# A Trainium2 transformer kernel: 1/rms applied to what leaves the products, and norms in a written order

## The chip, the cores and the metric

One program on one core of a Trainium2 chip. The metric is the device time in microseconds of one execution. The runs of the kernel before have a median of 4474.64 us (4474.46 to 4476.37, three runs).

## What is computed

A residual stream of 1024 tokens by 1024 features goes through one transformer block and two further layers. The part that the change touches is the first block:

```python
def rms_norm(x, g):
    y = x * lax.rsqrt(jnp.mean(x * x, axis=-1, keepdims=True) + RMS_EPS)
    return y * g

def swiglu(x, w_gate, w_up, w_down):
    return (jax.nn.silu(x @ w_gate) * (x @ w_up)) @ w_down

f1 = swiglu(rms_norm(x, ffn1_pre_g), ffn1_w_gate, ffn1_w_up, ffn1_w_down)   # 1024 -> 2816 -> 1024
x = x + 0.5 * rms_norm(f1, ffn1_post_g)
m = token_mixer(rms_norm(x, mix_pre_g), w_in, fox_forget_b, ..., w_out)
x = x + rms_norm(m, mix_post_g)
f2 = swiglu(rms_norm(x, ffn2_pre_g), ffn2_w_gate, ffn2_w_up, ffn2_w_down)
x = x + 0.5 * rms_norm(f2, ffn2_post_g)
```

The token mixer projects the rows with `w_in` into queries, keys and values of eight heads with a forget gate and of four differential heads (two softmaxes each, the second subtracted with a factor lambda, partly rotated queries and keys), and into eight gate columns. The logarithm of the gate's sigmoid is summed up over the tokens and added to the logits of the first eight heads. The heads' outputs go through `w_out`. Behind the block come an even layer (a gated linear recurrence and a state space scan) and an odd layer (stick-breaking attention), which the change leaves alone.

## The kernel before, in words

**Layout.** Everything is feature-major: 1024 features are eight chunks k of 128 partitions, the 1024 tokens are columns in two halves c = 0, 1 of 512 (`HALVES`). `res` holds the residual stream (x, then y), `acc` a block's output, `xh` and `xl` the normalised rows as a high and a low half. Every product is three fp32r matmuls of 128x512 per chunk, high times high, low weight times high, high weight times low (`pe_product`, L417 to L419; in the mixer's projections L1032 to L1034), 24 matmuls for eight chunks.

**Weights.** They come as 286 units of 128x1024 in a fixed order. SyncE loads a unit into one of two `raw` buffers once the low half of the unit two before is made (`sp_weights`), ScalarE copies it to `whi` (L390, three buffers), GpSimd subtracts to `wlo` (L399), and TensorE waits for the low half before the unit's first product. ScalarE and GpSimd do this at places that are written into their programs (`act_units`, `pool_units`), between their other steps, and each engine runs its instructions strictly in its written order.

**Norms.** A norm is a chain (`Chain`, with a part on each engine: `chain_act`, `chain_pe`, `chain_dve`, `chain_pool`), one per token half. ScalarE squares the eight chunks (L456), TensorE sums each over the partitions with a matrix of ones (L496, eight accumulating matmuls), VectorE makes mean plus eps, ScalarE Ln and Exp, VectorE three steps of a root refinement (L523 to L529). Between two blocks there are two statistics: the first over the block's output `acc`, after which VectorE scales each chunk (L544) and adds it to `res` (L563 for even chunks on VectorE, L603 for odd ones on GpSimd); the second over the new `res`, after which VectorE makes `res` x gain x 1/rms (L581), ScalarE its high half `xh` (L479), and VectorE or GpSimd its low half `xl` (L585 for odd, L613 for even chunks). So the next product cannot begin before the second statistic is complete. `Steps` cuts the chains into steps, which an engine takes between its other work (`tick`) or all up to a point (`need`).

**Feed-forward.** `pe_ffn` goes over 22 j of 128 hidden features: for each j and half c a gate product into bank b and an up product into bank b + 1, and every second j the down products of the pair before (11 b, eight output chunks, two halves). ScalarE takes silu of the gate bank from PSUM (L785), VectorE multiplies it with the up bank (L809), ScalarE makes the high half (L789, `hh`), GpSimd the low half (L832, `hl`), VectorE adds the down products into `acc` (L818, L820). `ffn_places` sets the order for the three engines other than TensorE.

**Mixer.** `pe_mixer` starts with the gate columns (unit IN.24) of both halves; their chain on VectorE, min, max, scan, (L1517 to L1523) ends in the cumulative sum `mnc`, which TensorE transposes (L1187) before the heads begin. The order of the heads is a list (`MIXER`) of items such as logits, mixing product, maxima, total, root; projections (`project(t)`, three units by two halves for each of eight t, through bank 7) are drawn in between the items by `Fill`. ScalarE evicts a projection, k and q of t < 4 straight to a high half, with the low half by VectorE from the bank (L1425); for t >= 4 k and q go to a tile `mx` (L1265), from which rotation, high half and GpSimd's low half (L1621) are made. At the start GpSimd stores `res` to memory (two transfers to `rs_scratch`), since the heads use its place, and loads it back during the last heads. The output products of half 0 are drawn in between the last heads; those of half 1 are a pass of their own (the units OUT.0' to OUT.7'), copied by VectorE to `acc`, beside the chains of half 0.

Of the kernel before, what the change touches and what calls it, by code (L numbers as in the profile page):

```python
# [7 lines left out]
D = 1024  # L8
T1 = 1024
META = 16  # L10
# [126 lines left out]
class Eng:  # L137


    def __init__(self, x, S, K):  # L140
        self.x, self.S, self.K = x, S, K
        self.seen, self.banks, self.held = {}, {}, {}
        self.bg = []
        self.nsq = self.ntmp = self.nw = 0
# [60 lines left out]
class Buffers:  # L205


    def __init__(self, nc, ctx):
# [9 lines left out]
        self.lam = at("mlam", [256], F32, o)  # L218
# [14 lines left out]
        f0 = o  # L233

# [3 lines left out]
                  for n, (off, i) in enumerate((off, i) for off in (65536, 57344) for i in range(4))]  # L238
# [12 lines left out]
        self.mb = at("mb", [2, 512], F32, q0 + 36864)  # L251
# [377 lines left out]
def in_chains():  # L629
    return [Chain(("n1", c), c, (lambda k, c=c: (f"ld_x{c}{k // 2}", 0)), None, ("res", "ffn1_pre_g", c0, c1))  # L630
            for c, (c0, c1) in enumerate(HALVES)]


# [16 lines left out]
def ffn1_chains():  # L650
    return [Chain(("n2", c), c, (lambda k, c=c: ("dve_acc", (1, 10, k, c))),
                  ("acc", "ffn1_post_g", 0.5, c0, c1), ("res", "mix_pre_g", c0, c1),
                  ffn_gates(1), [("pe_group", ("u", 1, 21, 1))]) for c, (c0, c1) in enumerate(HALVES)]


def mixer_chains():
    return [Chain(("n3", c), c, (lambda k, c=c: ("dve_out", (k, c))),
                  ("acc", "mix_post_g", 1.0, c0, c1), ("res", "ffn2_pre_g", c0, c1),
                  [("pe_mix", ("mix", 95)), ("dve_mix", ("root", 7, 1))],
                  [("pe_group", ("out", 7, c))], back="mix") for c, (c0, c1) in enumerate(HALVES)]  # L660


# [8 lines left out]
def pe_ffn(pe, f, xt, made):  # L671
# [3 lines left out]
    def gate_up(j):  # L675
        ig, gh, gl = pe_unit(pe, f"G{f}.{j}")
        for c, (c0, c1) in enumerate(HALVES):
            b = 2 * ((2 * j + c) % 2)
            xt.need(c)
            tag = xt.tags[c]  # L680
            pe.bank(b)
            pe_product(pe, K.bank(b), 8, eight(K, gh, gl, c0, c1), ("g", f, j, c),
                       lambda k: pe.wait_ge(*split_key(tag, k)))
            pe.tick(5)
            iu, uh, ul = pe_unit(pe, f"U{f}.{j}")
            pe.bank(b + 1)
# [2819 lines left out]
```

## Time and profile before

| | |
|---|---|
| median of three runs | 4474.64 us |
| the profiled execution's time | 4472.5 us |
| its span | 4470.7 us |
| mean granted TensorE clock | 0.952 of full speed |
| TensorE busy | 4068.1 us (91%), 20614 matmuls |
| VectorE busy | 1767.6 us (40%), 2368 instructions |
| ScalarE busy | 1365.0 us (31%), 2105 instructions |
| GpSimd busy | 1536.7 us (34%), 943 instructions |
| chain that ended last, by engine | TensorE 76%, VectorE 13%, ScalarE 5%, issue 3%, GpSimd 2%, DMA 1% |
| DMA | 206.01 MB, 46 GB/s in the mean |

The span is the time from the first to the last instruction in the trace; the profiled execution's own time is a little longer. The chain that ended last is followed back from the last instruction, each time to what released it. The busy shares are means over stages that differ: on the time axis the first block lies at about 80 to 771 us, the mixer's heads at 931 to 1624, the second block at 1768 to 2460, and the two further layers behind it.

### The profile page before, as it was taken

How to read it: one execution, taken by the hardware profiler on the slowest of the kernel's cores; microseconds unless marked ns; L12 is line 12 of the kernel's file. 1: busy time of each engine (PE TensorE's matmuls, PEld its weight loads, DVE VectorE, ACT ScalarE, POOL GpSimd, SP SyncE). 2: the span in 40 equal slices, each digit the busy share in tenths (PEclk: the TensorE clock that was granted, in tenths of full speed). 3: DMA queues.
4: the chain of work that ended last, by engine and by line, in shares of the span. 5: the costliest groups of instructions: out<-in, count | busy, mean ns of one | idle time of the engine just before them, and what ended most of it. 6: DMA issues, size and time to landing. Idle time of an engine off the chain costs nothing.

```text
span 4470.7 us, 48684 instructions
## 1 busy us (share of the span) xinstructions
PE 4068.1 (91%) x20614; PEld 3245.2 (73%) x20614; DVE 1767.6 (40%) x2368; ACT 1365.0 (31%) x2105; POOL 1536.7 (34%) x943
## 2 busy tenths in 40 slices
PE   7999999499999897999999588899976889999998
PEld 5888887266565465888888388899855787888878
DVE  2221222534345534212212554444384304666664
ACT  3111112222222223111111343332222214666663
POOL 3232232222434443322232232332472223334454
PEclk9999999799999898999999789999997999999999
DMA  2111111010000110111111011121111030000113
GB/s 86 48 52 43 48 52 43 14 67 20 24 19 15 53 57 33 53 42 51 54 46 49 5 41 38 37 91 56 46 43 53 27 118 25 28 26 25 32 55 130
DMA packets 57176, 206.01 MB, mean 46 GB/s; under 512 B 7424, under 2 KB 11040, under 8 KB 56320
## 3 DMA queue, kind: packets, MB, share of 16 engines
q1 hardware_dynamic: 45744, 158.55, 10.6%
q0 software_dynamic: 8656, 41.75, 2.5%
q8 instruction: 162, 2.65, 0.2%
q10 hardware_dynamic: 2560, 2.61, 0.2%
q14 instruction: 54, 0.44, 0.0%
HBM read 177.40 MB, written 25.49 MB: 45 GB/s over the span
## 4 chain that ended last, share of the span: by engine, by line
PE 76%; DVE 13%; ACT 5%; issue 3%; POOL 2%; DMA 1%; DVEq 0%; ACTq 0%; POOLq 0%
PE ps L417 15%; PE ps L418 15%; PE ps L419 15%; PE ps L2756 3%; PE ps L496 3%; PE ps L2689 2%; PE ps L2691 2%; PE ps L2690 2%; PE ps L1032 2%; PE ps L1033 2%; PE ps L1034 2%; PE ps L2740 2%; PE ps L2786 2%; PE ps L1132 1%; PE ps L1103 1%
## 5 line engine op out<-in xcount | busy, mean ns | idle before, releaser
L417 PE MATMUL ps<-xh,whi 128*128 128x512 f32 (+2 forms) x2888 | 1059.8, 367 | 69.7 <-POOL xl L613 49.6
L418 PE MATMUL ps<-xh,wlo 128*128 128x512 f32 (+2 forms) x2888 | 1046.4, 362 | 0.0
L419 PE MATMUL ps<-xl,whi 128*128 128x512 f32 (+2 forms) x2888 | 1042.0, 361 | 0.0
L399 POOL TENSOR_TENSOR wlo<-raw,whi 128x1024 fp32r<-128x1024 f32 x286 | 691.8, 2426 | 802.5 <-ACT whi L390 802.5
L417 PEld LDWEIGHTS ps<-xh,whi 128*128 128x128 f32 x2888 | 550.4, 191 | 159.7 <-POOL xl L613 53.9
L418 PEld LDWEIGHTS ps<-xh,wlo 128*128 128x128 f32 x2888 | 549.9, 190 | 67.8 <-issue 2.6
L419 PEld LDWEIGHTS ps<-xl,whi 128*128 128x128 f32 x2888 | 549.8, 190 | 64.6
L390 ACT ACTIVATE whi<-raw 128x1024 fp32r<-128x1024 f32 x286 | 295.6, 1050 | 477.1 <-PE ps L419 438.9
L809 DVE TENSOR_TENSOR t<-ps,t 128x512 f32<-128x512 f32 x88 | 60.9, 692 | 890.0 <-PE ps L419 888.6
L832 POOL TENSOR_TENSOR hl<-t,hh 128x512 fp32r<-128x512 f32 x88 | 114.0, 1295 | 721.4 <-ACT hh L789 721.4
L3055 POOL TENSOR_TENSOR ospl<-osp,osph 128x672 fp32r<-128x672 f32 (+4 forms) x144 | 191.0, 1326 | 370.3 <-ACT osph L2871 369.4
L496 PE MATMUL ps<-t,mat 128*128 128x512 f32 (+2 forms) x352 | 170.6, 633 | 160.7 <-ACT t L456 154.3
L820 DVE TENSOR_TENSOR acc<-acc,ps 128x512 f32<-128x512 f32 x320 | 219.9, 687 | 217.9 <-PE ps L419 217.9
L417 PE MATMUL ps<-hh,whi 128*128 128x512 f32 x704 | 276.8, 393 | 0.0
L418 PE MATMUL ps<-hh,wlo 128*128 128x512 f32 x704 | 274.1, 389 | 0.0
L419 PE MATMUL ps<-hl,whi 128*128 128x512 f32 x704 | 274.0, 389 | 0.0
L496 PEld LDWEIGHTS ps<-t,mat 128*128 128x128 f32 x352 | 77.6, 231 | 239.4 <-ACT t L456 147.9
L2689 PE MATMUL ps<-xh,whi 128*128 128x352 f32 (+1 forms) x576 | 191.1, 332 | 25.7 <-DVE okl L2928 19.0
L789 ACT ACTIVATE hh<-t 128x512 fp32r<-128x512 f32 x88 | 55.8, 634 | 494.3 <-DVE t L809 494.3
L2691 PE MATMUL ps<-xl,whi 128*128 128x352 f32 (+1 forms) x576 | 186.3, 324 | 0.0
L2690 PE MATMUL ps<-xh,wlo 128*128 128x352 f32 (+1 forms) x576 | 186.2, 323 | 0.0
L613 POOL TENSOR_TENSOR xl<-t,xh 128x512 fp32r<-128x512 f32 (+2 forms) x60 | 63.9, 1066 | 310.5 <-ACT xh L479 310.5
(340 smaller groups left out, 6935.4 us busy)
## 6 DMA issues: line engine op xcount, KB each, us to landing
raw<-in_w_dram SPq DMA_DIRECT2D x286, 512.0 KB, 3.2
res<-rs_scratch POOLq DMA_DIRECT2D x16, 520.0 KB, 7.4
rs_scratch<-res POOLq DMA_DIRECT2D x2, 4160.0 KB, 13.6
rs_scratch<-res POOLq DMA_DIRECT2D x2, 2080.0 KB, 11.9
szin<-zs_scratch SPq DMA_DIRECT2D x8, 520.0 KB, 3.3
gs_scratch<-oot POOLq DMA_DIRECT2D x8, 520.0 KB, 5.6
og<-gs_scratch POOLq DMA_DIRECT2D x16, 176.0 KB, 2.6
oot<-rs_scratch POOLq DMA_DIRECT2D x2, 1408.0 KB, 8.3
```

The costliest lines, as they stand in the source:

```text
L390: act.x.activation(K.whi[n % 3][:, :], K.raw[n % 2][:, :], ACT.Copy).then_inc(*S.up("w_hi", n))
L399: pool.x.tensor_tensor(K.wlo[n % 3][:, :], K.raw[n % 2][:, :], K.whi[n % 3][:, :], ALU.subtract).then_inc(*S.up("w_lo", n))
L417: pe.x.matmul(out, wh, xh, start=k == 0, stop=False)
L418: pe.x.matmul(out, wl, xh, start=False, stop=False)
L419: last = pe.x.matmul(out, wh, xl, start=False, stop=k == K - 1)
L496: pe.x.matmul(K.bank(b, n), K.m("ones"), K.t[(0, 1, 6)[q % 3]][:, 0:n], start=k == 0, stop=k == ch.KT - 1, skip_group_check=True).then_inc ...
L820: dve.x.tensor_tensor(acc, acc, pp, ALU.add).then_inc(*S.up("dve_acc", (f, b, ft, c)))
L2689: pe.x.matmul(K.bank(7, c1 - c0), a, x, start=k == 0, stop=False)
L2690: pe.x.matmul(K.bank(7, c1 - c0), b_, x, start=False, stop=False)
L2691: last = pe.x.matmul(K.bank(7, c1 - c0), a, y, start=False, stop=k == 7)
L2756: last = pe.x.matmul(PS[:, (4 + i) * 512 + x0:(4 + i) * 512 + x1], mat[:, :], part[n % 2][:, i, 0:x1 - x0], start=first, stop=False, skip_ ...
L3055: pool.x.tensor_tensor(K.ospl[n % 2][:, :, 0:x1 - x0], K.osp[n % 2][:, :, 0:x1 - x0], K.osph[n % 2][:, :, 0:x1 - x0], ALU.subtract).then_i ...
```

## The change

In the two feed-forward blocks and the mixer, the rows that go into a product are now x times the gain only (`fxh`, `fxl`), and 1/rms, one number per token and so per column, multiplies the product when it leaves its bank. In the chain's place stands a class `Late` with functions that do one chunk each, and their order is written out per engine.

- **High and low half of a chunk** are made as soon as its `res` is there: `act_high` on ScalarE, `dve_low` on VectorE for all chunks. TensorE waits chunk by chunk (`pe_paced`), and takes the squares of the second statistic (`pe_square`) between the chunks of the first product.
- **Between the blocks** VectorE does scale (in place in `acc`, L802), addition (L807) and low half (L824) for every chunk; GpSimd does none of it.
- **1/rms** goes to `rs0` (half 0), to `rs1a` and `rs1b` (half 1, 256 columns each), and for the mixer to `t[2]` and `t[3]` (`dve_root`).
- **Feed-forward:** VectorE evicts gate and up by a multiplication with 1/rms (`scaled`, L985; two pieces of 256 columns for half 1), silu works in SBUF, and the multiplication (L1002) reads SBUF only.
- **Mixer:** every projection is evicted by VectorE with 1/rms into `mx` or `mvr`; k and q of all t get their high half from ScalarE and the low half from GpSimd. The gate columns are scaled by VectorE, then the bias is added. The gate product of half 1 stands behind the first four steps of `project(0)`.
- **Written orders** (`IntoMixer...` for block one into the mixer, `OUT_SUMS` and `OUT_ROWS` for the output pass of the mixer). Into the two further layers (`IntoChains`) the chains stay.
- **Spill and restore:** `res` is stored per token half, as soon as that half's last chunk is added; `mb` now lies in the place of chunks 6 and 7, and these two are loaded back behind the last root. Lambda is worked out at the start.

The diff, cut to its core:

```diff
+def eight1(K, wh, wl, c0, c1):
+    def part(k):
+        o = k * 128
+        return wh[:, o:o + 128], wl[:, o:o + 128], K.fxh[:, k, c0:c1], K.fxl[:, k, c0:c1]
+    return part
...
+def dve_apply(dve, L, k):
+    f, y = K.acc[:, k, L.cols[0]:L.cols[1]], rows_of(K, L, k)
+    dve.wait_ge("late_root", (L.tag, 0, "r"))
+    dve.x.scalar_tensor_tensor(f, f, K.v(L.post, k), norm_tiles(K, L)[1], ALU.mult, ALU.mult)...
+    if L.back:
+        dve.wait_ge(f"back{k}", L.back)
+    dve.wait_ge("late_a", (L.tag, k))
+    dve.x.tensor_tensor(y, y, f, ALU.add).then_inc(*S.up("late_y", (L.tag, k)))
+
+def act_high(act, L, k):
+    rows_ready(act, L, k)
...
+    act.x.activation(K.fxh[:, k, c0:c1], rows_of(K, L, k), ACT.Copy, scale=K.v(L.pre, k))...
+
+def dve_low(dve, L, k):
+    dve.wait_ge("late_hi", (L.tag, k))
+    dve.x.scalar_tensor_tensor(K.fxl[:, k, c0:c1], rows_of(K, L, k), K.v(L.pre, k), K.fxh[:, k, c0:c1],
+                               ALU.mult, ALU.subtract).then_inc(*S.up("late_lo", (L.tag, k)))
+
+def pe_paced(pe, L, st):
+    def wait(k):
+        pe.wait_ge("late_lo", (L.tag, k))
+        if st and k:
+            pe_square(pe, L, 1, k - 1)
+    return wait
...
 def dve_ffn(dve, f, norms, after):
+    def scaled(out, b, c, what, j):
+        pieces = side_tiles(K, c)
+        for i, (tile, o, n) in enumerate(pieces):
+            dve.x.tensor_tensor(out[:, o:o + n], K.bank(b)[:, o:o + n], tile[:, 0:n], ALU.mult)...
     def gate_up(j, c):
-        dve.wait_ge("act_ffn", ("silu", f, j, c))
+        dve.wait_ge("pe_group", ("g", f, j, c))
+        scaled(ea, b, c, "gs", j)
         dve.wait_ge("pe_group", ("u", f, j, c))
...
-        dve.x.tensor_tensor(eb, K.bank(b + 1), ea, ALU.mult)...
+        scaled(eb, b + 1, c, "us", j)
+        dve.wait_ge("act_ffn", ("silu", f, j, c))
+        dve.x.tensor_tensor(eb, eb, ea, ALU.mult)...
...
+class IntoMixerDve:
...
+    def end(self):
+        dve, (a, b) = self.dve, self.norms
+        for k in range(8):
+            dve_apply(dve, a, k)
+            if k:
+                dve_low(dve, a, k - 1)
+            if k == 3:
+                dve_variance(dve, b, 0)
+            if k == 5:
+                dve_root(dve, b, 0)
...
+OUT_SUMS = [[(0, 0, k) for k in range(4)],
+            [(0, 0, k) for k in range(4, 8)] + [(1, 0, 0)],
+            [(1, 0, 1)],
+            [(1, 0, 2), (0, 1, 0), (0, 1, 1)],
...
+OUT_ROWS = [[], [], [0, 1], [2, 3], [4, 5], [6], [7], []]
...
 def pe_mixer(pe, norms, after):
...
-    fill.work(16)
+    gate(0)
+    fill.work(4)
+    gate(1)
+    fill.work(12)
...
 def dve_mixer(dve, norms, after):
     def project(t):
...
+                    dve.x.scalar_tensor_tensor(K.mx[:, :], X, 0.125 if which == "q" else 1.0, K.t[2 + c][:, :],
+                                               ALU.mult, ALU.mult).then_inc(*S.up("dve_prj", ("in", t, which, c)))
...
 def pool_mixer(pool, A, norms):
-    for i in range(2):
-        pool.x.dma_start(A["rs"][:, 4 * i:4 * i + 4, :], K.res[:, 4 * i:4 * i + 4, :])...
+    for c, (c0, c1) in enumerate(((0, META + 512), (META + 512, T2))):
+        pool.wait_ge("late_y", (norms[c].tag, 7))
+        pool.x.dma_start(A["rs"][:, :, c0:c1], K.res[:, :, c0:c1]).then_inc(*S.up("spill", ("mix", c), 16))
```

How the order of the instructions moves, at three places. VectorE between block one and the mixer, half 0, before (`t_73` is the scaled chunk, `t_77` the scaled row, `t_74` and `t_72` the two 1/rms):

```order
L544 SCALAR_TENSOR_TENSOR t_73<-acc,vec,t_74 128x512
L563 TENSOR_TENSOR res<-res,t_73 128x512
L581 SCALAR_TENSOR_TENSOR t_77<-res,vec,t_72 128x512
L544 SCALAR_TENSOR_TENSOR t_73<-acc,vec,t_74 128x512
L581 SCALAR_TENSOR_TENSOR t_77<-res,vec,t_72 128x512
L585 TENSOR_TENSOR xl<-t_77,xh 128x512
```

The same place now (`t_82` is 1/rms of the first statistic, `t_81` the variance of the other half):

```order
L802 SCALAR_TENSOR_TENSOR acc<-acc,vec,t_82 128x512
L807 TENSOR_TENSOR res<-res,acc 128x512
L824 SCALAR_TENSOR_TENSOR fxl<-res,vec,fxh 128x512
L760 TENSOR_SCALAR t_81<-ps 128x512
L802 SCALAR_TENSOR_TENSOR acc<-acc,vec,t_82 128x512
L807 TENSOR_TENSOR res<-res,acc 128x512
L824 SCALAR_TENSOR_TENSOR fxl<-res,vec,fxh 128x512
```

Before, the scale and half of the additions and low halves stood here, with the row's scaling by the second 1/rms; now there are three instructions per chunk, all on VectorE, and none needs the second statistic.

TensorE at the mixer's first product, the gate columns of half 0, before (`t_71`, `t_76`, `t_70` hold squares, `mat` the ones):

```order
L496 MATMUL ps<-t_76,mat 128x512
L496 MATMUL ps<-t_70,mat 128x512
L496 MATMUL ps<-t_71,mat 128x512
L496 MATMUL ps<-t_76,mat 128x512
L417 MATMUL ps<-xh,whi_58 128x512
L418 MATMUL ps<-xh,wlo_61 128x512
L419 MATMUL ps<-xl,whi_58 128x512
```

The same place now (`t_84` to `t_86` hold squares):

```order
L747 MATMUL ps<-t_85,mat 128x512
L428 MATMUL ps<-fxh,whi_58 128x512
L429 MATMUL ps<-fxh,wlo_61 128x512
L430 MATMUL ps<-fxl,whi_58 128x512
L747 MATMUL ps<-t_86,mat 128x512
L428 MATMUL ps<-fxh,whi_58 128x512
L429 MATMUL ps<-fxh,wlo_61 128x512
L430 MATMUL ps<-fxl,whi_58 128x512
L747 MATMUL ps<-t_84,mat 128x512
```

The squares of the second statistic, which all stood ahead of the product, now alternate with its chunks.

VectorE in the body of a feed-forward block, one j of half 0 and one of half 1, before (`t_70` and `t_72` hold the silu) and below it now (`t_76` and `t_78` hold the scaled gate, `t_77` and `t_79` the scaled up):

```order
L809 TENSOR_TENSOR t_71<-ps,t_70 128x512
L809 TENSOR_TENSOR t_73<-ps,t_72 128x512
```

```order
L985 TENSOR_TENSOR t_76<-ps,rs_52 128x512
L985 TENSOR_TENSOR t_77<-ps,rs_52 128x512
L1002 TENSOR_TENSOR t_77<-t_77,t_76 128x512
L985 TENSOR_TENSOR t_78<-ps,rs1a 128x256
L985 TENSOR_TENSOR t_78<-ps,rs1b 128x256
L985 TENSOR_TENSOR t_79<-ps,rs1a 128x256
L985 TENSOR_TENSOR t_79<-ps,rs1b 128x256
L1002 TENSOR_TENSOR t_79<-t_79,t_78 128x512
```

Two instructions became eight, and the up bank's eviction now stands between the up product and the multiplication.

## Rows read from the trace of the kernel before

**Rows 1.** Busy time by stretch: us, PE, PEld, DVE, ACT, POOL, PEclk, DMA, GB/s

```profile
0.00:80.00 80.00, 49.11 (x155) 30.57 (x156) 26.74 (x37) 31.43 (x48) 26.17 (x23) 0.94 0.26 94
...
31.00:50.00 19.00, 10.59 (x18) 3.82 (x19) 11.87 (x17) 10.12 (x18) 5.08 (x4) 0.73 0.00 0
...
80.00:771.00 691.00, 691.00 (x3004) 563.40 (x3003) 144.61 (x210) 115.35 (x150) 202.92 (x105) 1.00 0.15 49
771.00:931.00 160.00, 96.28 (x319) 63.62 (x317) 73.92 (x92) 43.02 (x67) 35.03 (x23) 0.78 0.13 47
931.00:1624.00 693.00, 659.64 (x3104) 403.59 (x3104) 303.08 (x332) 194.52 (x294) 278.72 (x167) 0.97 0.08 28
1624.00:1768.00 144.00, 110.39 (x378) 74.13 (x379) 65.17 (x74) 46.67 (x71) 52.63 (x31) 0.91 0.12 41
```

**Rows 2.** TensorE's waits, 771 to 931 us: us in total, times, longest

```profile
PE ps L496 <- ACT t L456: 50.8, 2, 36.3
```

**Rows 3.** TensorE's waits, 1624 to 1768 us

```profile
PE ps L417 <- POOL wlo L399: 16.1, 5, 8.1
```

**Rows 4.** Timeline of the start: start, us, engine line op, [idle before <- releaser]

```profile
20.92 10.06 PE L496 MATMUL ps<-t,mat 128*128 128x512 f32 x16 [20.92 <-ACT t L456]
...
79.59 0.60 ACT L785 ACTIVATE t<-ps 128x512 f32<-128x512 f32 x1 [2.24 <-PE ps L419]
```

**Rows 5.** The input's four loads on ScalarE's queue (line 3271)

```profile
DMA to landing us min/median/max: 10.0/12.7/15.5
```

**Rows 6.** Timeline of block two, a hand-over of weights, ScalarE, VectorE, GpSimd

```profile
1845.40 0.60 ACT L785 ACTIVATE t<-ps 128x512 f32<-128x512 f32 x1 [4.14 <-PE ps L419]
...
1851.02 0.69 DVE L809 TENSOR_TENSOR t<-ps,t 128x512 f32<-128x512 f32 x1 [10.43 <-PE ps L419]
...
1852.46 1.30 POOL L832 TENSOR_TENSOR hl<-t,hh 128x512 fp32r<-128x512 f32 x1 [9.83 <-ACT hh L789]
1853.73 4.74 POOL L399 TENSOR_TENSOR wlo<-raw,whi 128x1024 fp32r<-128x1024 f32 x2
...
1856.52 0.60 ACT L785 ACTIVATE t<-ps 128x512 f32<-128x512 f32 x1 [2.25 <-PE ps L419]
```

**Rows 7.** Timeline, mixer into block two, TensorE and ScalarE

```profile
1624.36 0.50 PE L417 MATMUL ps<-xh,whi 128*128 128x512 f32 x1 [1.31 <-POOL wlo L399]
...
1630.02 4.45 PE L496 MATMUL ps<-t,mat 128*128 128x512 f32 x10
...
1767.96 0.60 ACT L785 ACTIVATE t<-ps 128x512 f32<-128x512 f32 x1 [2.23 <-PE ps L419]
```

**Rows 8.** Timeline, block one into the mixer, VectorE and GpSimd

```profile
789.58 1.70 POOL L603 TENSOR_TENSOR res<-res,t 128x512 f32<-128x512 f32 x1 [22.89 <-DVE t L544]
...
790.20 1.63 DVE L563 TENSOR_TENSOR res<-res,t 128x512 f32<-128x512 f32 x1
...
827.03 0.74 DVE L544 SCALAR_TENSOR_TENSOR t<-acc,vec,t 128x512 f32<-128x512 f32 x1
827.81 0.69 DVE L563 TENSOR_TENSOR res<-res,t 128x512 f32<-128x512 f32 x1
828.42 0.74 DVE L581 SCALAR_TENSOR_TENSOR t<-res,vec,t 128x512 f32<-128x512 f32 x1
829.08 0.74 DVE L544 SCALAR_TENSOR_TENSOR t<-acc,vec,t 128x512 f32<-128x512 f32 x1
```

**Rows 9.** Timeline, the gate columns' chain, VectorE and TensorE

```profile
906.96 0.68 DVE L1517 TENSOR_SCALAR me<-mz 72x1024 f32<-72x1024 f32 x1
...
914.75 3.55 PE L1187 MATMUL ps<-mat,mnc 8*128 8x8 f32 x16 [3.67 <-DVE mnc L1523]
```

**Rows 10.** The chain that ended last: the store of the residual stream

```profile
890.45 14.52 DMA rs_scratch<-res
```

**Rows 11.** Timeline, mixer, the tile mx, GpSimd and ScalarE

```profile
1354.72 1.27 POOL L1621 TENSOR_TENSOR mkl<-mx,mkh 128x512 fp32r<-128x512 f32 x1 [1.53 <-ACT mkh L1306]
...
1360.97 0.58 ACT L1265 ACTIVATE mx<-ps 128x512 f32<-128x512 f32 x1
```

More of the change, by code:

```diff
@@ new lines, in act_square, with pe_square @@
+def act_square(act, L, st, k):
+    S, K = act.S, act.K
+    q = act.nlate
+    act.nlate += 1
+    if st:
+        rows_ready(act, L, k)
+        src = rows_of(K, L, k)
+    else:
+        act.wait_ge(*L.ready(k))
+        src = K.acc[:, k, L.cols[0]:L.cols[1]]
+    if k == 0:
+        for g in L.gates:
+            act.wait_ge(*g)
+    if q >= 3:
+        act.wait_ge("pe_late", q - 3)
+    act.x.activation(K.t[8 + q % 3][:, :], src, ACT.Square).then_inc(*S.up("late_sq", q))
+def pe_square(pe, L, st, k):
+    S, K = pe.S, pe.K
+    q = pe.nlate
+    pe.nlate += 1
+    b = L.banks[st]
+    pe.wait_ge("late_sq", q)
+    if k == 0:
+        pe.bank(b)
+    pe.x.matmul(K.bank(b), K.m("ones"), K.t[8 + q % 3][:, :], start=k == 0, stop=k == 7,
+                skip_group_check=True).then_inc(*S.up("pe_late", q))
+    if k == 7:
+        S["pe_late"].vals[(L.tag, st)] = S["pe_late"].n
+        pe.banks[b] = [("late_root", (L.tag, st, "v"))]
@@ L726, in pe_ffn @@
         down_group(10, 0, ft, wh, wl)
-    out = made(pe, "pe")
+    after.begin()
     for ft in range(8):
@@ L732, in pe_ffn, with ffn_places @@
             S.freed[i] = "pe_group", ("d", f, 10, ft, 1)
-    out.open = len(out.gens)
-    return out
-def ffn_places(e, f, xt, gate_up, down_group, units, made, which, before=None):
+        after.beside(ft)
+    after.end()
+def ffn_places(e, f, gate_up, down_group, units, after):
     def at_gate_up(j):
@@ new lines, in dve_in, with __init__, begin, beside @@
+def dve_in(dve, norms):
+    for L in norms:
+        for k in range(8):
+            dve_low(dve, L, k)
+            if L.c and k == 3:
+                dve_variance(dve, norms[0], 1)
+            if L.c and k == 5:
+                dve_root(dve, norms[0], 1)
+    dve_variance(dve, norms[1], 1)
+    dve_root(dve, norms[1], 1)
+class IntoMixerPE:
+    def __init__(self, pe, norms):
+        self.pe, self.norms = pe, norms
+    def begin(self):
+        pass
+    def beside(self, ft):
+        if ft < 4:
+            pe_square(self.pe, self.norms[0], 0, 2 * ft)
+            pe_square(self.pe, self.norms[0], 0, 2 * ft + 1)
+    def end(self):
+        for k in range(8):
+            pe_square(self.pe, self.norms[1], 0, k)
@@ new lines, with __init__, begin, beside @@
+class IntoMixerAct:
+    def __init__(self, act, norms):
+        self.act, self.norms = act, norms
+    def begin(self):
+        exp_ln(self.act)
+    def beside(self, ft):
+        pass
+    def end(self):
+        act, (a, b) = self.act, self.norms
+        act_units(act, UNIT_AT["IN.24"])
+        for k in range(8):
+            act_square(act, a, 0, k)
+        act_root(act, a, 0)
+        for k in range(8):
+            act_square(act, b, 0, k)
+        act_units(act, UNIT_AT["IN.24"] + 1)
+        for k in range(8):
+            act_high(act, a, k)
+            act_square(act, a, 1, k)
+            if k == 3:
+                act_root(act, b, 0)
+        act_units(act, UNIT_AT["IN.24"] + 2)
+        for k in range(8):
+            act_high(act, b, k)
+            act_square(act, b, 1, k)
+            if k == 3:
+                act_root(act, a, 1)
+        act_root(act, b, 1)
@@ L1037, in project @@
                 last.then_inc(*S.up("pe_prj", (t, which, c)))
[L1038 removed]
+                pe.banks[b] = [("dve_prj", ("in", t, which, c))]
                 if c:
@@ L1048, in rows @@
             pe.bank(7)
-            part = eight(K, wh, wl, c0, c1)
+            part = eight1(K, wh, wl, c0, c1)
             for k in range(8):
```

536 lines of the change are left out of this document (339 added, 197 removed), and 4 rows, old and new, of the table OUT_SUMS.

## The prediction

> **What bounds the kernel now.** I read the stretches first [rows 1]. In feed-forward block one TensorE is busy for all of 691 us at full granted clock, and block two reads the same: there only a new wait can change the time. The attention stretch (931 to 1624) is 95% busy. What is left is three hand-overs: the start (49.11 of 80 us busy), block one into the mixer (96.28 of 160, granted clock 0.78) and mixer into block two (110.39 of 144). Together 128 us of TensorE idle (30.9 + 63.7 + 33.6). The waits name the cause. At the first hand-over TensorE waits 50.8 us for squares from ScalarE, 36.3 of them at once [rows 2]; at the second 16.1 us for weight halves, since GpSimd and ScalarE sit in the norm's steps in between [rows 3]. So TensorE is idle because a product's rows need 1/rms, which needs the sum over all eight chunks. The change removes that need, and the sum is made from these three places, less what the new work costs in the body.
>
> **Start.** TensorE begins at 20.92 with squares (8 in 10.06 us), and the first gate product of the second j ends at 79.5, where a silu waiting for it starts [rows 4]. The input pieces of ScalarE's queue land 10.0 to 15.5 us after their issue [rows 5], at 2.2 to 3.9 us, and in the new order ScalarE no longer makes a third weight unit first. I take 14.5 us for the first matmul. Until that gate product ends TensorE does five products and 16 squares. A product is half the 11.12 us between two silus [rows 6], 5.56 us; a square is two records of the trace, and ten in 4.45 us make it 0.89 [rows 7]. 5 x 5.56 + 16 x 0.89 = 42.0. The clock granted fell to 0.73 of full speed between 31 and 50 us, behind the first squares [rows 1]; the other of its two levels is half of full speed, 1.2 GHz. Some of that will stay, so I add 5, and 2 for the first hand-over of weights: 63.5. Gain 79.5 - 63.5, **16 us**. Bounds: the first matmul only at 20.92, 9; no slow phase, 21.
>
> **Block one into the mixer.** VectorE now does all of it: per chunk acc x g x r (0.78 to the next start), y + f (0.61), low half (0.66) [rows 8], 2.05 us, 16 chunks = 32.8. It starts when the last accumulation of the block ends, about 789.8. To it come a variance and three root steps of 0.7 us for two of the statistics, 5.8; 2 for ScalarE, which has 8 squares of half 1 in front of the first high half; 2 for the port (below). The low halves end at 832.4. After: high and square of the last chunk, variance, Ln and Exp, root 6.3; the gate rows' two scalings and the bias 2.3, and the first k tile through mx to its low half and the second into mx 3.5 (both estimates, from instructions of 0.7 and 1.27 us); and the old chain from min to cumulative sum 7.7 (906.96 to 914.7) [rows 9]. Cumulative sum at about 853 against 914.75: 61. TensorE does gate(1), with the k and q products (3 x 5.56) after it, beside this and is warm, where before it ran 16 products of 8 columns in 3.55 us and was slow after: 2.5 more. Gain **63.5 us**. The spill to memory does not bound: it was 14.52 us for both halves behind each other [rows 10]; now half 0 goes 20 us earlier, and half 1 alone lands before 843, even at the whole old duration. Bounds: each y + f at 1.63 instead of 0.69 [rows 8] costs 16 x 0.94 = 15 us (gain 48); ScalarE's and the port's extras at nothing, 68.
>
> **Mixer into block two.** The order of the change puts 23 squares between the eight output products, so that ScalarE and GpSimd reach each weight unit in time. The pass began at 1624.36 [rows 7]. The late restore adds two GpSimd issues ahead of the weight half that TensorE waits for there; they also wait for the last attention root, but what stands before them did so already. I take 1.1 us. 1625.5 + 8 x 5.56 + 23 x 0.89 + 3.5 of waits = 1694. Gate and up of half 0 run at once. Half 1's gate waits for its low halves: two roots 6.7, 8 x 2.05, 0.7, so 23.8; square, variance, roots to 30; then evictions, mul, high, low and the next weight half to 39, so the second up product starts at 1733 against 1768, where the silu after its gate product starts [rows 7]. Gain **35 us**. Bounds: the 16.1 us of weight waits come back, 20; the 3.5 us and 1.1 us vanish, 40.
>
> **The blocks' body.** 88 (j, half) pairs get two evictions on VectorE from PSUM, half 1 in two pieces of 256 columns each. VectorE was busy 144.61 of 691 us [rows 1], so the work is hidden, apart from one place: after the last up product of an odd j the chain runs mul, hh, weight high, hl, weight low. The up eviction now stands ahead of mul, two pieces, 0.8 us (an estimate, between the 0.69 of one whole instruction and twice that). The chain in the old trace: mul 1851.02, weight low 1853.73, first of two done 2.37 later, 1856.1; the product that needs it begins at 1856.3, since the silu at 1856.52 follows its predecessor [rows 6]. Slack 0.2, so 0.6 us is exposed, 10 times in each block: **-12 us**. Bounds: 0.2 each (-4), 1.2 each (-24). Here banks 0 to 3 come free one product or more before need, and the eviction of gate runs under up. ScalarE's silu moves from PSUM to SBUF, same size, no effect.
>
> **Mixer body.** 48 projection evictions go to VectorE (16 were there already: +32 x 0.69 = 22 us on an engine at 303 of 693 [rows 1]), 16 low halves to GpSimd. mx is a single buffer: VectorE waits for the low half before, and its maxima queue behind it; ScalarE's exps then queue behind high. In the old trace that low half starts at 1354.72 and takes 1.27, and the next copy into mx starts at 1360.97 [rows 11]: five us of slack. What the added k and q evictions do to the heads' own steps on VectorE, which stand in one queue with them, no row shows. Bank 7 comes free after one instruction instead of two, so I take **0**, -8 to +8.
>
> The one rule that speaks against it. Where y + f ran beside GpSimd's add, it took 1.63 us, and alone 0.69; GpSimd's took 1.70 [rows 8], where a subtraction of the same size beside nothing took 1.27 [rows 11]. The new low halves and the new mul read two SBUF operands too. In the stretches above GpSimd has only few weight halves (2.37 us), hence 2 us. In the blocks, mul starts after up products, when GpSimd is idle in the old trace [rows 6]. The Trainium skill (SBUF — State Buffer, Who interferes with whom) states that a VectorE instruction with two SBUF inputs contends with a GpSimd one that reads SBUF, and the loser blocks fully; the old mul had one SBUF input. By that rule this case's 1.63 is a queued instruction, and the trace agrees; were every y + f blocked so, the sum would be 15 us worse.
>
> **Sum.** 16 + 63.5 + 35 - 12 + 0 = 102.5. The profiled execution took 4472.5 us (span 4470.7), so 4370; the median of the runs, 4474.64, is 2.1 us above it, so I say **4372 us**.
>
> **Rivals.**
> - *VectorE's chain becomes the wait.* Low halves come every 2.05 us, TensorE needs 0.70 + 0.89 per chunk: it waits in gate(0) and gate(1), and anything more per chunk counts 16 times in one hand-over, 8 in the other. At 3 us a chunk: 23 us less gain, 4395. For: VectorE has all three steps, where GpSimd had a share. Against: the rows above are from the same steps. 0.22. My forecast: 0.62.
> - *The port in the body.* If weight halves run when mul comes after an odd j, the whole handover waits up to 2.37 us: 20 x 2.4 = 48, and 8 in the hand-overs: 4428. Against: [rows 6] show hl and weight low after mul in that order. By the Trainium skill's rule above it would come so if mul were pushed late. 0.09.
> - *The time gained is lost again*, by weight units arriving late throughout: within 0.2%. 0.03.
> - *Slower: mx.* Each of 32 k and q evictions makes VectorE wait for GpSimd's low half; behind an add (2.4) and a weight half (2.37) it comes 6 us later, TensorE stands at bank 7, ScalarE at high. It outweighs the 102.5 us from 3.2 us per eviction on; at 6 it costs 192: 4564. Against: the five us of slack. 0.04.
>
> **Numbers.** The likeliest case stands at 4372. Its bounds, taken together as independent, are some 20 us each way; with the first rival and a part of the second the range is 4349 to 4402. What a measurement of this kernel tells from no change is 0.2%, 9 us. Faster 0.94, same 0.02, slower 0.04.
>
> **What would show it.** Right: gate product of the first j from about 15 us, its squares between chunks; cumulative sum some 61 us earlier after the block's end; no TensorE wait on weight halves in the output pass; twenty waits of about 0.6 us on weight low in the blocks. Wrong: TensorE waits on fxl of over 25 us in one hand-over; waits of over 1 us in the blocks' body; attention longer than 701 us between the first k.q matmul and the output pass.

## The result

The changed kernel takes 4360.9 us (median of four runs, 4360.5 to 4363.6) where the kernel before takes 4475.5 (four runs): ratio 0.9745, 95% interval 0.9728 to 0.9762, 115 us less. The forecast was 4372 with a range of 4349 to 4402. It held, but partly by luck: a gain of some 27 us that no step of the forecast had made up for several steps that were a few us too kind.

The profiled execution took 4363.6 us, with a span of 4361.7 against 4470.7 before: the comparison of stretches below adds up to these 109.0 us.

Busy time by stretch of the changed kernel, with the bounds moved to the same places of the program as in [rows 1] (columns as there):

```profile
0.00:67.00 67.00, 47.40 (x159) 31.52 (x160) 27.01 (x43) 32.60 (x50) 17.81 (x15) 1.00 0.32 115
67.00:757.00 690.00, 683.54 (x2996) 562.20 (x2995) 203.33 (x335) 116.49 (x149) 201.66 (x105) 1.00 0.15 49
757.00:863.00 106.00, 94.02 (x334) 63.34 (x332) 65.64 (x92) 41.86 (x64) 19.64 (x12) 0.94 0.21 75
863.00:1560.00 697.00, 660.71 (x3121) 408.87 (x3122) 344.02 (x363) 177.59 (x264) 292.98 (x179) 0.97 0.09 29
1560.00:1700.00 140.00, 134.33 (x529) 98.44 (x528) 68.89 (x98) 53.19 (x79) 38.26 (x19) 1.00 0.15 49
```

Block one into the mixer lasted 160 us and is 106 now, with TensorE idle for 12 instead of 64. In the body of block one TensorE now idles for 6.5 us, which it did not before. TensorE's waits in the four stretches, in this order: block one's body, the hand-over into the mixer, the heads (the largest one), the output pass into block two. Each line gives us in total, times, longest.

```profile
PE ps L428 <- POOL wlo L402: 6.5, 11, 0.6
...
PE ps L747 <- DVE fxl L824: 6.9, 6, 2.3
PE ps L1584 <- DVE mnc L1892: 2.9, 1, 2.9
PE ps L428 <- DVE fxl L824: 2.2, 1, 2.2
...
PE ps L1505 <- DVE mdg L1825: 13.7, 7, 2.9
...
PE ps L428 <- POOL wlo L402: 3.1, 2, 2.5
PE ps L428 <- DVE t L985: 1.7, 1, 1.7
PE ps L747 <- DVE fxl L824: 0.9, 4, 0.2
```

The wait of 50.8 us for squares [rows 2] and that of 16.1 for weight halves in the output pass [rows 3] are gone. To compare stretches I use marks that both programs have: the first down product of each block, the last one, the transposes of the cumulative sum, and the first product of the output pass. The gains are us of the two profiled executions. The last column is what a_rows4160 takes more than the changed kernel, a run of the changed kernel with the row spacing of the kernel before (below); each of its rows is one profile against another, and in the heads most of it turns out to be the granted clock (below).

| stretch | forecast gain | measured gain | of it the rows' spacing |
|---|---|---|---|
| start to the first down product | 16 | 12.5 | 0.9 |
| block one, to its last down product | -6 | 0.8 | 8.3 |
| to the transposes of the cumulative sum | 61 | 56.1 | 0.2 |
| the heads, to the output pass | 2.5 | 2.7 | 7.5 |
| output pass, to block two's first down product | 35 | 37.6 | 1.6 |
| block two, to its last down product | -6 | 0.8 | 8.2 |
| the rest | 0 | -1.5 | -1.3 |
| sum | 102.5 | 109.0 | 25.3 |

The first surprise stands in the second row: the waits for weight halves were forecast and are there (eleven in the block, ten of them between these marks), and yet the block is no longer than before. The rows of the marks, TensorE in the timeline, before:

```profile
118.35 0.39 PE L417 MATMUL ps<-hh,whi 128*128 128x512 f32 x1
...
758.97 0.39 PE L417 MATMUL ps<-hh,whi 128*128 128x512 f32 x1
```

and in the changed kernel:

```profile
105.87 0.39 PE L428 MATMUL ps<-hh,whi 128*128 128x512 f32 x1
...
744.89 0.39 PE L428 MATMUL ps<-hh,whi 128*128 128x512 f32 x1
```

640.6 us from the first down product to the beginning of the last pair of down units before, 639.0 now, though nine waits lie in between. Within a gate or up product the 24 matmuls begin 231.6 ns apart before and 227 now (5.56 and 5.44 us for the 24, medians of block one), at full granted clock in both. Down products run at the same pace in both. One thing of the change touches just those rows: they lay 4160 bytes apart per chunk (1040 columns), and now lie 4096 apart (1024 columns).

### The profile page after: what moved, and what is told of

Same layout as the page of the kernel before. It is cut to its first block, busy times and chain, and to the rows that moved or that the text cites. A ratio compares the mean times of both kernels' runs of the same rounds, so it can differ in the third digit from the quotient of the medians.

```text
span 4361.7 us, 49059 instructions
## 1 busy us (share of the span) xinstructions
PE 4032.6 (92%) x20614; PEld 3239.2 (74%) x20614; DVE 1914.3 (44%) x2659; ACT 1350.2 (31%) x2072; POOL 1500.5 (34%) x919
## 4 chain that ended last, share of the span: by engine, by line
PE 75%; DVE 13%; ACT 5%; POOL 4%; issue 3%; DMA 1%; DVEq 0%; ACTq 0%; POOLq 0%
PE ps L428 14%; PE ps L429 14%; PE ps L430 14%; PE ps L3118 3%; PE ps L3051 2%; PE ps L1426 2%; POOL wlo L402 2%; PE ps L3053 2%; PE ps L3052 2%; PE ps L1427 2%; PE ps L1428 2%; PE ps L3102 2%; PE ps L3148 2%; PE ps L1526 1%; PE ps L1497 1%
## 5 line engine op out<-in xcount | busy, mean ns | idle before, releaser
L428 PE MATMUL ps<-fxh,whi 128*128 128x512 f32 x1488 | 604.4, 406 | 38.9 <-POOL wlo L402 19.3
L429 PE MATMUL ps<-fxh,wlo 128*128 128x512 f32 x1488 | 581.0, 390 | 0.0
L430 PE MATMUL ps<-fxl,whi 128*128 128x512 f32 x1488 | 580.8, 390 | 0.0
L428 PE MATMUL ps<-xh,whi 128*128 128x352 f32 (+1 forms) x1400 | 466.6, 333 | 32.5 <-POOL xl L624 28.8
L428 PEld LDWEIGHTS ps<-fxh,whi 128*128 128x128 f32 x1488 | 280.5, 189 | 118.0 <-issue 33.2
L429 PEld LDWEIGHTS ps<-fxh,wlo 128*128 128x128 f32 x1488 | 280.6, 189 | 67.8 <-issue 12.1
L430 PEld LDWEIGHTS ps<-fxl,whi 128*128 128x128 f32 x1488 | 280.4, 188 | 59.2
L428 PEld LDWEIGHTS ps<-xh,whi 128*128 128x128 f32 x1400 | 268.6, 192 | 44.2 <-POOL xl L624 27.7
L429 PEld LDWEIGHTS ps<-xh,wlo 128*128 128x128 f32 x1400 | 268.3, 192 | 2.6 <-issue 0.9
L430 PEld LDWEIGHTS ps<-xl,whi 128*128 128x128 f32 x1400 | 268.1, 192 | 0.0
L985 DVE TENSOR_TENSOR t<-ps,rs 128x512 f32<-128x512 f32 x88 | 60.7, 691 | 401.1 <-PE ps L430 401.1
L3051 PE MATMUL ps<-xh,whi 128*128 128x352 f32 (+1 forms) x576 | 191.2, 332 | 25.9 <-DVE okl L3290 19.1
```

The source lines that it names most:

```text
L428: pe.x.matmul(out, wh, xh, start=k == 0, stop=False)
L429: pe.x.matmul(out, wl, xh, start=False, stop=False)
L430: last = pe.x.matmul(out, wh, xl, start=False, stop=k == K - 1)
L3051: pe.x.matmul(K.bank(7, c1 - c0), a, x, start=k == 0, stop=False)
```

## The experiments

**The rows' spacing, alone, in the kernel before.**

```diff
+        self.fxh, self.fxl = at("fxh", [8, T1], F32R, x0 + 0), at("fxl", [8, T1], F32R, x0 + 32768 + 0)
...
-            pe_product(pe, K.bank(b), 8, eight(K, gh, gl, c0, c1), ("g", f, j, c),
+            pe_product(pe, K.bank(b), 8, eight1(K, gh, gl, c0, c1), ("g", f, j, c),
```

(`eight1` takes the rows from `fxh` and `fxl`; likewise in the other products of the transformer block, in its norms and in the output rows of the mixer.)

> The kernel before, with one thing of the change: the rows of the first block's products (xh, xl) lie 4096 bytes apart per chunk instead of 4160. In the traces a gate or up product of 24 matmuls takes 5.56 us before and 5.44 after. Theory A, the spacing of the rows in SBUF is the cause: 242 products of 24 matmuls with some 5 ns less each, 176 of them in the two feed-forward blocks; 21 us if only those count, 29 if all do, so 4446 to 4454 us, and a product takes 5.44. Theory B, the faster product comes from what the other engines do beside it (evictions instead of silu from the bank, other tiles): no change, 4475, product 5.56.

4450.2 us against 4476.9 before, ratio 0.9942 (0.9927 to 0.9957). The time from the first down product to the last pair of down units is 631.6 us instead of 640.6:

```profile
116.94 0.39 PE L418 MATMUL ps<-hh,whi 128*128 128x512 f32 x1
...
748.52 0.39 PE L418 MATMUL ps<-hh,whi 128*128 128x512 f32 x1
```

A product takes 5.44 us. Theory A holds: the profiled executions differ by 19.0 us of span (the medians by 26.7), and 18.1 of these lie in the two blocks' bodies. The heads gained nothing here (709.8 against 709.6).

**The same rows, moved by 64, 128 and 192 bytes.**

```diff
-        self.fxh, self.fxl = at("fxh", [8, T1], F32R, x0 + 0), at("fxl", [8, T1], F32R, x0 + 32768 + 0)
+        self.fxh, self.fxl = at("fxh", [8, T1], F32R, x0 + 64), at("fxl", [8, T1], F32R, x0 + 32768 + 64)
```

> As b_rows4096, with both tiles moved by 64 bytes, so that each chunk's rows begin 128 bytes past a multiple of 256 instead of 64 past it (before, the chunks went through all four such places). If where a row begins counts, the product differs from the 5.44 us of b_rows4096, up to the slowest chunk before, 3 x 233 ns, that is 5.59 for eight. If only the spacing counts, it is 5.44 again.

> As b_rows4096 (a product of 5.44 us) and b_rows4096_off64 (5.49), moved by 128 bytes, so that a chunk's rows begin 192 past a multiple of 256. If the place modulo 128 counts, it is 5.44 again; if modulo 256, another value, up to 5.56.

> As b_rows4096, moved by 192 bytes: a chunk's rows begin at a multiple of 256. The products took 5.44 us at 64 bytes past it, 5.49 at 128, 5.59 at 192. If a round start is what TensorE wants, 5.44 or less; if there is no such order, anything between 5.44 and 5.59.

The product takes 5.49, 5.59 and 5.60 us; the times, of one run each, are 4457.8, 4478.3 and 4475.7. Two silus in the timeline, two products apart, moved by 64 (10.99 us):

```profile
287.66 0.60 ACT L797 ACTIVATE t<-ps 128x512 f32<-128x512 f32 x1 [4.08 <-PE ps L420]
298.65 0.60 ACT L797 ACTIVATE t<-ps 128x512 f32<-128x512 f32 x1 [2.19 <-PE ps L420]
```

and by 192 (11.20 us):

```profile
289.69 0.60 ACT L797 ACTIVATE t<-ps 128x512 f32<-128x512 f32 x1 [4.18 <-PE ps L420]
300.89 0.60 ACT L797 ACTIVATE t<-ps 128x512 f32<-128x512 f32 x1 [2.29 <-PE ps L420]
```

`x0` lies 64 bytes past a multiple of 256, so the four starts, b_rows4096's among them, are 64, 128, 192 and 0 past one. It is then not the spacing of 4096 as such that makes the product fast: where a chunk's rows begin counts. 64 bytes past a multiple of 256 is the best of the four; 192 past it and the multiple itself are the slowest, and these two are not told apart. With 4160 the chunks go through all four places and lie in between (5.56). The place alone does not give that figure: the mean of the four is 5.53, and a chunk at 64 takes 690 ns in the mix where it takes 680 in b_rows4096. The four kernels differ only in this offset. Within a product the spacing of the matmuls follows the place too: moved by 64, every chunk has 231, 226 and 229 ns; moved by 192, 234, 233 and 233. Why is open; the weights' tiles did not move, and I did not try those.

**The old spacing in the changed kernel.**

```diff
-        self.fxh, self.fxl = at("fxh", [8, T1], F32R, x0), at("fxl", [8, T1], F32R, x0 + 32768)
-        self.rs1 = [at("rs1a", [256], F32, x0 + 65536), at("rs1b", [256], F32, f0 + 73728)]
...
+        self.fxh, self.fxl = self.xh, self.xl
+        self.rs1 = [at("rs1b", [256], F32, f0 + 73728)] * 2
...
```

> The changed kernel with the spacing of the kernel before for fxh and fxl, 4160 bytes. For want of room the first half of half 1's 1/rms is left out (both pieces use the second 256 columns); the instructions are the same. Theory A: the product takes 5.56 us again, the time rises by 21 to 29 us to 4382 to 4390. Theory B: 4361 as the changed kernel.

4387.7 us, ratio to before 0.98 (0.9785 to 0.9814), 27 us above the changed kernel. What the change does apart from the tile's shape is thus worth 89 us, not 115. The forecast for that part was 102.5, so it was some 13 too high (19 by the spans of the two profiles, 5 of them the granted clock in the heads, below). That part fell short in the start, the hand-over into the mixer and the heads.

**Up's eviction left out.**

```diff
-        scaled(eb, b + 1, c, "us", j)
         dve.wait_ge("act_ffn", ("silu", f, j, c))
-        dve.wait_ge("dve_ffn", ("us", f, j, c))
-        dve.x.tensor_tensor(eb, eb, ea, ALU.mult)
+        dve.x.tensor_tensor(eb, K.bank(b + 1), ea, ALU.mult)
```

> The changed kernel without the eviction of up: the multiplication reads the up bank in PSUM and the scaled gate's silu, so 1/rms of the up half is left out. If the two pieces of that eviction make the 22 waits of 0.59 us on the weights' low half, these shrink to the old slack, nothing or under 0.1 us each: 12 to 13 us less, 4348. If the waits come from elsewhere (the silu, or the low halves of the rows ahead in GpSimd's order), they stay: 4361.

4340.0 us, 21 less than the changed kernel, where 12 to 13 were expected. None of the eleven waits in block one's body is left. From the first down product to the last pair of down units the body takes 631.4 us, 7.65 less for nine waits, and the last down products 0.9 less for one: a wait of 0.59 us costs about 0.85. One of them in the changed kernel:

```profile
88.44 0.39 PE L430 MATMUL ps<-fxl,whi 128*128 128x512 f32 x1
89.41 0.50 PE L428 MATMUL ps<-fxh,whi 128*128 128x512 f32 x1 [0.59 <-POOL wlo L402]
89.75 0.39 PE L429 MATMUL ps<-fxh,wlo 128*128 128x512 f32 x1
```

In the stream a matmul begins 0.23 us after the one before, at 0.39 us each. Behind the wait one begins 0.97 after, that is 0.74 late, and the next 0.34 after, another 0.11. The rest of the gain, 2.1 us at the start (0.85 of it the wait shown, which lies ahead of the first mark) and 2.5 in the two hand-overs, was not expected; there, too, weights come earlier.

**Weights ahead of hh and hl.**

```diff
 act_ffn, gate_up(j, c), behind the silu
+        if c:
+            act_units(act, UNIT_AT[f"U{f}.{j}"] + 2)
         act.wait_ge("dve_ffn", ("mul", f, j, c))
...
 pool_ffn, gate_up(j, c)
+        if c:
+            pool_units(pool, UNIT_AT[f"U{f}.{j}"] + 2)
         pool.wait_ge("act_ffn", ("hh", f, j, c))
```

> The changed kernel; for half 1 of each j, ScalarE makes the next weight's high half between silu and hh, and GpSimd its low half before hl. In the changed kernel both stand behind hh and hl, which wait for the multiplication and so for both evictions of up. If the waits of 0.59 us are only this order, they go (17 us for both blocks, as leaving out the eviction gave 7.65 + 0.9 each), and the wait of 2.5 us for the weights of the second j's up product at both block starts shrinks by 2 each: 4340. Rival: the weight halves now take GpSimd when hl or the multiplication wants it, TensorE waits on hl or hh instead: nothing gained, 4361 or more.

4339.2 us, ratio to before 0.9691 (0.9677 to 0.9706), as forecast. TensorE in the timeline of the changed kernel, the long wait at the block's start and the first of the eleven:

```profile
65.16 0.50 PE L428 MATMUL ps<-fxh,whi 128*128 128x512 f32 x1 [2.54 <-POOL wlo L402]
...
89.41 0.50 PE L428 MATMUL ps<-fxh,whi 128*128 128x512 f32 x1 [0.59 <-POOL wlo L402]
```

and in this kernel the first, the only one left of its kind in block one:

```profile
62.77 0.50 PE L428 MATMUL ps<-fxh,whi 128*128 128x512 f32 x1 [0.44 <-POOL wlo L402]
```

Since it can be made earlier here, the weight had not waited for a buffer; it stood behind hh, which stood behind two evictions and a multiplication. So the cost that the change puts on the body is a matter of order, and was avoidable in full: the two bodies gain 8.9 each, and the start 4.9. From the first down product to the last pair of down units block one takes 631.0 us, against 631.6 in b_rows4096, which has neither the evictions nor the waits.

**Weight halves moved away from VectorE's two-input instructions.** The changed kernel, VectorE in the timeline:

```profile
53.34 2.50 DVE L793 SCALAR_TENSOR_TENSOR rs1a<-t,t 128x256 f32<-128x256 f32 x1
55.76 0.41 DVE L793 SCALAR_TENSOR_TENSOR rs1b<-t,t 128x256 f32<-128x256 f32 x1
...
781.30 2.33 DVE L824 SCALAR_TENSOR_TENSOR fxl<-res,vec,fxh 128x512 fp32r<-128x512 f32 x1 [2.58 <-ACT fxh L816]
...
784.94 0.74 DVE L824 SCALAR_TENSOR_TENSOR fxl<-res,vec,fxh 128x512 fp32r<-128x512 f32 x1
...
800.78 2.87 DVE L802 SCALAR_TENSOR_TENSOR acc<-acc,vec,t 128x512 f32<-128x512 f32 x1
...
1646.16 2.49 DVE L793 SCALAR_TENSOR_TENSOR rs1a<-t,t 128x256 f32<-128x256 f32 x1
```

and GpSimd:

```profile
52.89 2.67 POOL L402 TENSOR_TENSOR wlo<-raw,whi 128x1024 fp32r<-128x1024 f32 x1 [36.72 <-ACT whi L393]
...
780.73 2.35 POOL L402 TENSOR_TENSOR wlo<-raw,whi 128x1024 fp32r<-128x1024 f32 x1 [27.34 <-ACT whi L393]
...
800.23 2.87 POOL L402 TENSOR_TENSOR wlo<-raw,whi 128x1024 fp32r<-128x1024 f32 x1 [17.15 <-ACT whi L393]
...
1645.71 2.67 POOL L402 TENSOR_TENSOR wlo<-raw,whi 128x1024 fp32r<-128x1024 f32 x1 [31.56 <-ACT whi L393]
```

Four times here an instruction of VectorE with two tiles of SBUF as input begins while a weight half runs on GpSimd, and ends 0.3 to 0.6 us after it: 781.30 + 2.33 = 783.63, GpSimd's end 783.08. There are more of them, which the edit below leaves as they are: a low half at the start (14.31 us, 2.41 long), one in the output pass (1591.82 us, 2.18 long) and many in the heads.

```diff
 act_in
+            if L.c and k == 3:
+                act_units(act, UNIT_AT["G1.1"])
...
 IntoMixerAct.end
+        act_units(act, UNIT_AT["IN.24"] + 1)
         act_root(act, a, 0)
         for k in range(8):
             act_square(act, b, 0, k)
-        act_units(act, UNIT_AT["IN.24"] + 1)
...
+        act_units(act, UNIT_AT["IN.24"] + 2)
         act_root(act, b, 1)
...
 act_out_end
+    act_units(act, UNIT_AT["G2.1"])
     act_root(act, b, 1)
```

(the second unit's earlier place is taken away, and GpSimd's part of it goes behind the two stores of the residual stream.)

> The changed kernel; five of its weight halves are moved to where VectorE is idle or reads one tile of SBUF: the second gate unit of both blocks ahead of the last root, and both units behind the gate columns, one ahead of the first root and one behind the last high half. In the changed kernel four instructions of VectorE with two SBUF inputs that begin beside such a low half took 2.33, 2.87, 2.50 and 2.49 us, where alone they take 0.74 and 0.42. If they wait for GpSimd, they now take 0.74 and 0.42, the block starts gain 2 us each and the hand-over into the mixer 4 to 5: 4352. If their length has another reason (the first write to a tile), they stay and nothing is gained: 4361.

4357.4 us (4352.5 to 4359.7); the profiled execution's span is 4350.6. VectorE in the timeline, the same four instructions (53.83 is the second half of the first):

```profile
53.48 0.42 DVE L793 SCALAR_TENSOR_TENSOR rs1a<-t,t 128x256 f32<-128x256 f32 x1
53.83 0.42 DVE L793 SCALAR_TENSOR_TENSOR rs1b<-t,t 128x256 f32<-128x256 f32 x1
...
776.87 0.75 DVE L824 SCALAR_TENSOR_TENSOR fxl<-res,vec,fxh 128x512 fp32r<-128x512 f32 x1 [1.63 <-ACT fxh L816]
...
794.77 0.74 DVE L802 SCALAR_TENSOR_TENSOR acc<-acc,vec,t 128x512 f32<-128x512 f32 x1
...
1638.59 0.43 DVE L793 SCALAR_TENSOR_TENSOR rs1a<-t,t 128x256 f32<-128x256 f32 x1
```

They wait for GpSimd, and not for a first write. The Trainium skill (SBUF — State Buffer, Who interferes with whom) states this as a rule, full blocking included, and the trace agrees. The start gained 3.5 us and the hand-over into the mixer 3.7. Block two's beginning lost 0.8: there TensorE now waits 3.7 us in one place for a weight half. Of the median's 3.5 us less than the changed kernel, little is beyond its own scatter of 7, and of the 11.2 us by which the profiled span is shorter 4.4 lie behind block two's last down product, where the edit changes nothing; the marks, not the total, carry this verdict. The 4352 expected were not reached.

**Both, and the first high half earlier.**

```diff
 IntoMixerAct.end
         for k in range(8):
             act_square(act, b, 0, k)
+            if k == 3:
+                act_high(act, a, 0)
```

> Both of a_weight_first and a_clear, and in the hand-over the first high half of half 0 stands behind four of the other half's squares, not eight. If the parts add: 21 + 9 + 1 = 31 us, 4330. If they overlap at the block starts, 4334. If one part undoes the other (weights earlier, beside the multiplication again), 4340 to 4350.

4329.8 us (4327.9 to 4334.8), ratio to before 0.9672 (0.9658 to 0.9687), 31 us under the changed kernel: the fastest kernel of this study. It leaves no part out. TensorE's only wait between 60 and 745 us:

```profile
PE ps L428 <- POOL wlo L402: 0.3, 1, 0.3
```

The start gains 6.7 us and the hand-over into the mixer 2.9, less than the 3.7 of a_clear alone. I did not look into why the parts don't add there.

**The mixer's evictions on ScalarE.**

```diff
 act_mixer, project(t)
+                act.x.activation(dst[:, :], X, ACT.Copy,
+                                 scale=0.125 if which == "q" else 1.0)...
 dve_mixer, project(t)
-                    dve.x.scalar_tensor_tensor(K.mx[:, :], X, 0.125 if which == "q" else 1.0, K.t[2 + c][:, :], ...
```

> The changed kernel with the mixer's 48 evictions of projections on ScalarE, as plain copies; 1/rms of these rows is left out. With the old spacing of rows (a_rows4160) the heads, from the transposes of the cumulative sum to the output pass, took 714.5 us against 709.6 before, so something there costs 5 us, or 7 if TensorE at its higher clock behind the transposes is worth the 2.5 I gave it. If it is the evictions standing in VectorE's queue ahead of the maxima and diagonals, that stretch falls from 707.0 to some 700 to 702, and the time to 4355. If ScalarE's queue pays as much (its exponentials behind evictions), it stays at 707 and 4361. The waits of VectorE on GpSimd's low halves of mx, the rival on the slower side, are nil in the trace, so they can give nothing.

4367.1 us, and the heads take 711.8 us, 4.8 more than in the changed kernel. The time is neither of the two expected, 4355 and 4361, and moving the evictions to ScalarE gives nothing back. TensorE's largest wait there is nearly the same with both:

```profile
PE ps L1505 <- DVE mdg L1825: 12.6, 7, 2.7
```

against 13.7 in the changed kernel. Nor does TensorE as a whole wait longer: its waits in the heads add up to 32.3 us before, 32.7 in a_rows4160 and 33.6 in the changed kernel.

The profiles show where most of the 5 us lie, by which the heads are longer in a_rows4160 than before at equal spacing of rows (714.5 against 709.6): in the granted clock. The first 230 us of the heads, before and in a_rows4160 (PEclk is the number ahead of the last two):

```profile
914.75:1144.75 230.00, 223.36 (x1114) 139.66 (x1114) 84.72 (x98) 56.85 (x97) 68.51 (x39) 0.96 0.06 21
...
854.71:1084.71 230.00, 220.45 (x1078) 139.21 (x1080) 98.39 (x103) 53.16 (x90) 81.16 (x50) 0.93 0.07 21
```

Over the whole stretch the granted clock was at the lower of its two levels, half, for 54 us before, 65 in a_rows4160, 54 in the changed kernel, 62 in b_rows4096 and 61 in a_mix_act. Taking half of that off each length, an estimate of the stretch at the full clock, gives 682.5, 682.0, 679.9, 678.8 and 681.1 us. So at equal spacing the change costs the heads nothing that can be seen; the spacing is worth 2 to 4 us there in both kernels, instead of 7.5 in the one and nothing in the other; and a_mix_act lies 1 us above the changed kernel. Why the clock was lower for longer in some of them is open. All these are single profiles, and in four kernels before with other row starts the stretch came out between 707.9 and 714.1.

## Why the prediction was right, and where it was not

**What bounded the kernel** was read right. The three places where rows waited for 1/rms gave 12.5 + 56.1 + 37.6 = 106 us of the 109.

**Start: 16 forecast, 12.5 measured.** Data came as taken, the first matmul at 14.09 us against 14.5. The five products and 16 squares ended at 62.6 against 63.5, so up to there the sum held. Its 7 us of extras were right in size and came from other places: the first three chunks took some 3 us more than later ones, with matmuls 0.43 us apart instead of 0.23, though the profile grants 1.00 there (why is open):

```profile
14.65 0.63 PE L429 MATMUL ps<-fxh,wlo 128*128 128x512 f32 x1
15.08 0.63 PE L430 MATMUL ps<-fxl,whi 128*128 128x512 f32 x1
```

waits for low halves took 1.3, and one for the first eviction 1.7. What failed is what comes next, which the step did not price: the up product of the second j waits 2.5 us for its weight half, which stands behind the first hh, and behind the wait matmuls begin 0.43 us apart for 3.4 us, at the clock's lower level (granted 0.51 from 66.65 to 70.10 us). a_weight_first gave 4.9 back.

**Block one into the mixer: 61 forecast to the transposes, 56.1 measured.** The terms of the forecast add up to 852.2 us for the cumulative sum, not 853, and so to 62.5, not 61. VectorE's chunk takes 2.05 us as worked out:

```profile
785.60 0.74 DVE L802 SCALAR_TENSOR_TENSOR acc<-acc,vec,t 128x512 f32<-128x512 f32 x1
786.38 0.69 DVE L807 TENSOR_TENSOR res<-res,acc 128x512 f32<-128x512 f32 x1
786.99 0.74 DVE L824 SCALAR_TENSOR_TENSOR fxl<-res,vec,fxh 128x512 fp32r<-128x512 f32 x1
787.65 0.68 DVE L760 TENSOR_SCALAR t<-ps 128x512 f32<-128x512 f32 x1
```

From 785.60 to 787.65 is the whole chunk. The terms that were small were those around it: the idle time for ScalarE's eight squares 2.6 instead of 2, the port 3.7 instead of 2, a wait of 1.1 for a root that had no term, the last root 8.3 us behind the last low half instead of 6.3, since TensorE has half of gate(1) left then, and the gate columns' chain 15 instead of 13.5.

**The heads: the 2.5 us for a warm TensorE are wrong.** The 16 small matmuls stand where they stood and take the same 3.55 us, and behind them TensorE is as slow as before:

```profile
845.37 3.55 PE L1584 MATMUL ps<-mat,mnc 8*128 8x8 f32 x16 [2.86 <-DVE mnc L1892]
848.85 0.80 PE L1426 MATMUL ps<-fxh,whi 128*128 128x512 f32 x1
849.44 0.63 PE L1427 MATMUL ps<-fxh,wlo 128*128 128x512 f32 x1
```

Work ahead of them did not help. The body's 0 plus or minus 8 holds: -5 at equal spacing, and about 0 with the granted clock taken out.

What went unseen there is the port. VectorE's 64 diagonals, the instruction that TensorE waits for most, take 0.42 us alone; 31 of them ran beside GpSimd and took longer, where it was 16 before. All 64 before and now (us in total, ns of one):

```profile
L1456 DVE SCALAR_TENSOR_TENSOR mdg<-mat,msm 128x256 fp32r<-128x256 f32 x64 | 43.6, 681 | 2.2
...
L1825 DVE SCALAR_TENSOR_TENSOR mdg<-mat,msm 128x256 fp32r<-128x256 f32 x64 | 59.4, 928 | 2.2
```

Every one that took over 0.52 us began while GpSimd ran an instruction. TensorE's wait for them rose from 10.4 us to 13.7; its other waits in the heads gave 2.0 of that back.

**Mixer into block two: 35 forecast, 37.6 measured**, 36 at equal spacing. The restore's 1.1 us are 1.2 (the first output product waits 2.51 us, it was 1.31 [rows 7]); the waits for weights in the pass itself, for which I had 3.5, are gone. The wait at the block's start, unpriced as in the start, came here too (2.51 us).

**Body: the mechanism was right, and the number of waits nearly**: ten of 0.59 us and an eleventh of 0.60 ahead of the last down unit, against ten of 0.6. Left out of the sum: what TensorE loses beyond the idle time of each wait (8.5 us for ten waits instead of 6), and the faster products (8 to 9 us a block the other way). The step that failed is the tacit one, that a product of the same shape takes the same time in both kernels.

**The rivals.** VectorE's chain as the wait: TensorE waits 9.1 us for low halves in the hand-over (6.9 ahead of squares and 2.2 ahead of the first product), as forecast in kind, at 2.05 us a chunk and not 3. The port in the body: none of the 88 multiplications met a weight half, which began 2.7 us or more behind the start of each; the port struck in the hand-overs, at the block starts and in the heads. The slower side, mx: VectorE was not once seen to wait for GpSimd's low half before such an eviction in the heads, only for the product itself. Its whole list of waits on that line there:

```profile
DVE mx L1795 <- PE ps L1428: 47.9, 19, 9.9
```

## What to carry to other kernels

Where a norm's factor is one number per column of the product, take it out of the rows and put it on the eviction: what then remains on the path is the work per chunk. When an instruction is put ahead of another on an in-order queue, look at all that queues behind, weights above all; a step that needs only a free buffer does not belong behind one that needs a result. And when a tile changes shape or place, compare the pace of the matmuls that read it, before crediting the gain to the idea.

## What the runs showed that I had not expected

- The pace of 128x512 fp32r matmuls depends on where in SBUF the moving rows begin: 24 matmuls took 5.44 us with rows 64 bytes past a multiple of 256, 5.49 at 128, and 5.59 to 5.60 at 192 and at 0, all at full granted clock. In this kernel the best against a mix of the four is 27 us of 4475 by the medians, 19 by the profiled spans.
- A wait that the profile shows as 0.59 us costs TensorE about 0.85: matmuls overlap in the stream, which the idle time does not count, and the one after the first behind it is 0.11 us late again.
- The same 64 instructions of VectorE took 0.68 us in the mean before and 0.93 now, since 31 instead of 16 of them began while GpSimd ran an instruction.
